# Hybrid block pair on one core: where the next head's query is split in a turn of the windowed attention

## The reference, cut to what matters

```python
def windowed_gqa_with_sink(q, k, v, sink):
    ...
    scores = jnp.einsum('bnqhrd,bnkhd->bnhrqk', qb, kb).astype(jnp.float32) * (ATTN_HEAD_DIM ** -0.5)
    ...
    scores = jnp.where(valid[None, :, None, None], scores, -jnp.inf)
    ...
    probs = jax.nn.softmax(jnp.concatenate([scores, sink_col], axis=-1), axis=-1)[..., :-1]
    out = jnp.einsum('bnhrqk,bnkhd->bnqhrd', probs.astype(v.dtype), vb)
```

## Time and profile before

| | |
|---|---|
| time, median of 3 runs | 2353.67 us (2353.35 to 2355.12) |
| time of the profiled execution | 2353.92 us |
| its span, first to last instruction | 2352.1 us |
| TensorE matmul busy | 2324.1 us, 99% |
| TensorE weight load busy | 2014.4 us, 86% |
| VectorE busy | 1636.3 us, 70% |
| ScalarE busy | 1243.7 us, 53% |
| GpSimd busy | 262.4 us, 11% |
| granted TensorE clock, mean | 0.999 |

### The profile page before, as it was taken

How to read it: one execution, slowest core, us unless ns; L and a number is a source line. 1 busy time by engine, 2 the same in 40 slices (tenths; PEclk the granted TensorE clock), 3 DMA queues, 4 the chain that set the end, 5 groups by cost and what they waited for, 6 DMA issues and landing times.

```text
span 2352.1 us, 35281 instructions
## 1 busy us (share of the span) xinstructions
PE 2324.1 (99%) x14088; PEld 2014.4 (86%) x14088; DVE 1636.3 (70%) x2353; ACT 1243.7 (53%) x2026; POOL 262.4 (11%) x208
## 2 busy tenths in 40 slices
PE   8999999999999999999999999999999999999998
PEld 7778778777788888899988899998887888899997
DVE  5698845478865455687785788785677565777784
ACT  7777765346663344455554555554544354555552
POOL 0000000465100100100002200001122201100002
PEclk9999999999999999999999999999999999999999
DMA  6221236324666232233233233223322232333222
GB/s 200 81 73 52 88 103 206 103 95 121 204 214 213 88 118 75 81 116 100 90 99 110 86 119 108 90 81 113 110 64 63 90 117 72 108 108 106 87 76 91
DMA packets 177844, 254.05 MB, mean 108 GB/s; under 512 B 10000, under 2 KB 101392, under 8 KB 177680
## 3 DMA queue, kind: packets, MB, share of 16 engines
q1 hardware_dynamic: 176528, 250.22, 33.1%
q10 hardware_dynamic: 1152, 1.57, 0.2%
HBM read 233.93 MB, written 16.78 MB: 107 GB/s over the span
## 4 chain that ended last, share of the span: by engine, by line
PE 93%; DVE 3%; ACT 2%; issue 1%; DMA 0%; POOL 0%; DVEq 0%; SPq 0%; POOLq 0%
PE bank L1492 92%; DVE wlo L2523 1%; PE bank L1660 1%; ACT whi L1899 0%; PE bank L1683 0%; PE bank L1781 0%; PE bank L1805 0%; DVE T L2531 0%; DVE W L2523 0%; DMA zb<-scr_z 0%; ACT E L2163 0%; DVE bank L2842 0%; DMA raw<-in_w_in 0%; PE bank L1618 0%; DVE xg L2527 0%
## 5 line engine op out<-in xcount | busy, mean ns | idle before, releaser
L1492 PE MATMUL bank<-xopr,shi 128*128 128x256 f32 x3360 | 605.0, 283 | 0.0
L1492 PEld LDWEIGHTS bank<-xopr,shi 128*128 128x128 f32 x3360 | 524.5, 192 | 0.5
L1492 PE MATMUL bank<-xopr,slo 128*128 128x256 f32 x1680 | 475.4, 283 | 0.0
L2523 DVE TENSOR_TENSOR wlo<-raw,whi 128x1024 fp32r<-128x1024 f32 (+2 forms) x286 | 354.6, 1244 | 140.8 <-ACT whi L1899 140.2
L1492 PE MATMUL bank<-xh,whi 128*128 128x512 f32 x1016 | 408.0, 402 | 7.4 <-DVE wlo L2523 7.4
L1492 PE MATMUL bank<-xh,wlo 128*128 128x512 f32 x1016 | 397.5, 391 | 0.0
L1492 PE MATMUL bank<-xl,whi 128*128 128x512 f32 x1016 | 397.2, 391 | 0.0
L1899 ACT ACTIVATE whi<-raw 128x1024 fp32r<-128x1024 f32 (+2 forms) x286 | 292.8, 1031 | 136.1 <-PE bank L1492 121.0
L1492 PEld LDWEIGHTS bank<-xopr,slo 128*128 128x128 f32 x1680 | 322.5, 192 | 0.0
L1492 PEld LDWEIGHTS bank<-xh,whi 128*128 128x128 f32 x1016 | 191.5, 188 | 50.0 <-DVE wlo L2523 8.2
L1492 PEld LDWEIGHTS bank<-xh,wlo 128*128 128x128 f32 x1016 | 191.1, 188 | 41.6
(11 more groups left out here) (398 smaller groups left out, 4320.7 us busy)
## 6 DMA issues: line engine op xcount, KB each, us to landing
raw<-in_w_in SPq DMA_DIRECT2D x92, 512.0 KB, 3.5
quarter<-in_w_ffn_in SPq DMA_DIRECT2D x32, 512.0 KB, 4.5
quarter<-in_ffn_gate SPq DMA_DIRECT2D x32, 512.0 KB, 3.6
quarter<-in_ffn_up SPq DMA_DIRECT2D x32, 512.0 KB, 4.6
raw<-in_ffn_down SPq DMA_DIRECT2D x28, 512.0 KB, 4.2
raw<-in_w_xattn_kv SPq DMA_DIRECT2D x16, 512.0 KB, 4.5
raw<-in_w_kv_mem SPq DMA_DIRECT2D x16, 512.0 KB, 4.9
raw<-in_w_branch_ssd SPq DMA_DIRECT2D x16, 512.0 KB, 4.6
```

The source lines that it names most:

```text
L1492: return e.matmul(out, l, r, start=start, stop=stop, skip_group_check=skip)
L2523: return e.tensor_tensor(out, a, b, op)
```

## The change

In each of the turns 0 to 14, the step `q_split(i + 1)` is taken out from behind `score_max(i, 1)` and `shift(i)` and put right behind `scores(i, 0)`. It stays the same step with the same instructions.

```diff
@@ -633,6 +633,8 @@
                         for r in (2 * pair, 2 * pair + 1):
                             side.new("sc", i, r)
                         step("scores", i, pair)
+                        if pair == 0 and i < 15:
+                            step("q_split", i + 1)
                     if i and pair == 0:
                         step("p_norm", last)
                     if i and pair:
@@ -644,8 +646,6 @@
                             step("shift", i)
                         elif i < 3:
                             step("k_split", i + 1)
-                    if pair and i < 15:
-                        step("q_split", i + 1)
                     if i:
                         side.new("pt", last, pair)
                         step("p_turn", last, pair)
```

## The result

The changed kernel takes 2356.86 us (median of 22 runs, 2355.25 to 2358.76). The kernel before takes 2353.84 us in 22 runs taken beside them. They reach from 2351.96 to 2355.12 us, with a single one far off at 3848.86 us, which can't move a median and which the ratio leaves out. The ratio is 1.0013, 95% interval 1.0007 to 1.0019: 1.6 to 4.5 us lost. That is real, and less than the 0.2% that I had set as the bound. The profiled execution took 2358.76 us, its span is 2356.1 us, and the clock's mean is 0.999.

What follows compares the result with a forecast made beforehand. TensorE's matmuls, busy 99% of the span, bound the kernel. Prices 0.83 + 0.75 + 0.41 + 0.83 + 0.38 = 3.2 us gave 2357.1 from the profiled execution, 2356.9 against the median; range 2353.9 to 2360.0.

Steps and rivals of the forecast that it cites:

- Turn 0: Attention's turn 0: ScalarE waits 6.18 us for TensorE behind the split's new place, which hides the split; no cost.
- Turn 1: Split ahead of ScalarE's normalisation delays it; transposition wait grows from 1.15 to 1.98 us, next stays 1.63; price 0.83 us.
- Turn 2: First maximum 1.58 us late, TensorE only 0.83, no room before second pair's scores; price 0.75 us, bounds 0 and 0.85.
- Turn 7: Transposition waiting for the normalisation: split costs 0.83, turn 6's removed split gives 0.42 back; price 0.41 us, bounds 0 and 0.83.
- Turn 10: Later normalisation delays VectorE's maximum; transposition's wait for its bank grows from 0.81 to 1.64 us; price 0.83, bounds 0 and 0.85.
- Turn 11: Same path as turn 10, 0.83 us late against 0.45 us of room at second pair's load; price 0.38, bounds 0 and 0.83.
- The other turns: Nine turns priced at nothing; hardest is turn 4, where 3.05 us of room hides VectorE's lag of 2.16 us.
- Slower: VectorE's waits for the high half exceed the room in turns 3 to 6, 8, 9: 5.1 us more, 2362.0; chance 0.18.
- Nothing to be seen on TensorE: Only turn 1's 0.83 us is lost; VectorE's gain behind shift covers the split at the other four places: 2354.5; chance 0.12.
- Faster: Earlier exponential and work behind it shrink the existing waits; at best 2349.7 us, short of 0.2%; chance 0.03.
- 3.97 us of existing waits: Weight-load idle times in the kernel before, in turns 1, 7 and 10: 1.15 + 1.63 + 0.38 + 0.81 us.
- The clock: Turn 1's wait of about 2 us drops TensorE's clock to 1.2 GHz, costing 5 us more: 2361.9; chance 0.02.

Runs made afterwards that it cites:

- ten_turns: Kernel before, with the split moved in turns 0, 3, 4, 5, 6, 8, 9, 12, 13 and 14 alone: 2353.40 us, ratio 0.9996.
- two_splits: Kernel before, with turn 1's split behind turn 0's first scores and turn 2's split behind shift(0): 2353.92 us, ratio 1.0001.
- five_turns: Kernel before, with the split moved in turns 1, 2, 7, 10 and 11 alone: 2358.22 us, ratio 1.0018.
- high_only: Kernel before, with only ScalarE's copies of the split moved in all 15 turns, VectorE's subtractions left behind shift: 2356.71 us, ratio 1.0010.
- two_ahead: Kernel before, with turns 1 and 2's splits in turn 0, turn 1's first maximum early, turn 0's normalisation directly behind its exponentials: 2356.04 us, ratio 1.0007.
- early_max: Kernel before, with only turn 1's first-pair maximum moved, right behind its scores: 2354.69 us, ratio 1.0003.
- behind_norm: Changed kernel, but with the split behind the normalisation instead of ahead of it: 2361.82 us (5 runs), ratio 1.0032.
- the last kernels: Kernel before with turns 1 and 2's splits in turn 0, without and with turns 6 and 9's splits also moved: 2353.92 and 2353.93 us.

## Why the prediction was right

**The time.** 2356.9 us predicted, 2356.86 measured. That they agree to 0.04 us is partly luck, since the medians of before themselves lie between 2353.67 and 2354.27. The sum is the better test: 3.20 us predicted, 3.27 in the ledger.

**Turn 0**, priced at nothing: its moved split is hidden, and even gives 0.13 us back at 87.36. ten_turns shows this alone (turn 0 moved, turn 1 not). two_splits puts a second split into turn 0, again at no cost.

**Turn 1**, 0.83 us: 0.86 by itself (five_turns), less turn 0's 0.13 gives the 0.73 in the table. The wait ahead of the transposition is 1.88 where I said near 2.0, the next one is unchanged as said. Behind it 0.13 us came back ahead of `scores(2, 0)`, where the wait for `pt` before `pv(0)` could shrink a little. I had left that out.

**Turn 2**, 0.75 us: 0.97, above my upper bound of 0.85. The maximum's delay was right: 109.65 against 107.38 less the start-up's 0.64 is 1.63 us, where I had 1.58. What I had too large was TensorE's own delay, which I set against it: 0.83, where the ledger stood at 0.73 - 0.13 = 0.60. The exponential waits 0.80 us for `shift` as I said. The cause is shown by high_only, where the subtractions stay and the jump is gone.

**Turn 7**, 0.41 us: 0.38, and both parts of the difference are shown: the split costs 0.81 alone (five_turns), and turn 6's moved subtractions give 0.43 back. In ten_turns, where only the giving back is left, it is worth 0.15, though the load idled 0.38. TensorE's matmuls in the kernel before say why:

```profile
202.03 0.39 PE L1492 MATMUL bank<-xl,whi 128*128 128x512 f32 x1
202.26 0.39 PE L1492 MATMUL bank<-xh,wlo 128*128 128x512 f32 x1
202.63 0.63 PE L1660 MATMUL bank<-cst,pr 128*128 128x128 f32 x4
```

The load idled beside a running matmul. The matmuls start 0.23 us apart, and this one came after 0.37: the wait was worth 0.14 us. The idle time of a load tells how a wait grows, but overstates what it costs. Turn 1's two waits, 1.15 and 1.63 us at the load:

```profile
86.22 0.39 PE L1492 MATMUL bank<-xh,wlo 128*128 128x512 f32 x1
87.36 0.63 PE L1660 MATMUL bank<-cst,pr 128*128 128x128 f32 x4 [0.75 <-ACT pr L1900]
...
90.35 0.39 PE L1492 MATMUL bank<-xh,wlo 128*128 128x512 f32 x1
91.98 0.58 PE L1492 MATMUL bank<-kh,qp 128*128 128x384 f32 x2 [1.24 <-DVE st L2663]
```

They are worth 87.36 - 86.22 - 0.23 = 0.91 us and 91.98 - 90.35 - 0.23 = 1.40 us, and two_ahead and early_max, which took them away, show just -0.90 and -1.40 in the ledger.

**Turn 10**, 0.83 us: 0.14 + 0.69 = 0.83. In five_turns the cost shows as a wait for a slot's low half instead (1.76 us at the load of 261.06, 0.75 at the same load before), of which 0.13 comes off the later wait: 1.02 - 0.13 = 0.89. I had said that a wait for low halves would come off the one at 266.68. **Turn 11**, 0.38 us: 0.29, the same in all three kernels that move ScalarE's copies in turns 10 and 11.

**The other turns**, nothing: turn 3 cost 0.23, which I had not foreseen, and ten_turns shows 0.14 there too. VectorE's gain of 0.85 us behind `shift(2)` was to cover the split. It ends in the wait of 1.08 us for `whi` in the rows above, where the kernel before has none: ScalarE writes this `whi` behind the exponentials, and these start from the same `shift`, so it comes no earlier. I had argued so for turn 2 and did not look for it in turn 3. In turn 4 VectorE waits 1.64 us, where I had worked out 1.31, and with the work of 0.85 the lag of 2.49 is still under the room of 3.05; no jump.

**The rivals.** *Slower:* its mechanism exists, as behind_norm shows with five such places, but not at this position of the split. *Nothing to be seen on TensorE:* excluded by five jumps. *Faster:* ten_turns and the last kernels show how little there is, 0.1 to 0.3 us, because a shortened wait comes back as another. My 3.97 us of existing waits could not be right beside the earlier trace rows, where TensorE idles 2.73 us in the whole stretch. Counted from matmul to matmul as in turn 7, the four waits are worth 0.91, 1.40, 0.14 and 0.55 us, 3.0 in all. The list of waits also lacked two, 0.49 us at 99.46 for `pt` and 0.75 us at 256.99 for a low half. *The clock:* it didn't fall in the changed kernel, behind the wait of 1.88 us or elsewhere up to the last matmuls. By the Trainium skill's page "TensorE: Matmul & The Clock Gate", in its part on the HAM clock gate, idleness brings the half clock back, and behind_norm and two_ahead agree with that, with 0.33 us for a load of 0.19. My price of 5 us for it was too high: the traces show 1.6 and 1.5 us (behind_norm's two falls) and 1.5 (two_ahead's).

## What to carry to other kernels

To price a move, look at what stands behind it on every engine up to the next idle time, and ask which of it TensorE waits for; work added there costs its full length, once, and in a gap nothing. Price a wait by how far apart the matmuls start around it, and not by the idle time of the weight load. Where a saturated engine sets the pace, a wait that you take away comes back a little later, and if waits flow together into one the clock may fall and make it a loss. For differences of a few microseconds in 2350, compare the start times of one engine's steps between two traces, and take the start-up off every time that you compare: with it, the copy that two_ahead brought 0.31 us forward reads as 0.86. Medians of eleven runs gave intervals of 2 us to either side; the ledger placed 0.1 us.

## What the runs showed of the hardware

TensorE's granted clock fell behind waits that I had thought harmless. After load waits of 2.50 us (behind_norm) and 2.55 us (two_ahead) it read 0.53 and 0.50 in the worst window of 2 us, the level of 1.2 GHz, and was back at 1.00 or 0.91 within 4 us. Each fall cost 1.5 to 1.6 us.

The length of the wait alone doesn't decide it. After 1.63 and 1.88 us (the changed kernel) and 1.92 (early_max) the clock read 1.00, and so it did behind the waits of 1.94 us at 533.58 and 1.95 at 641.29 in the changed kernel. But in behind_norm it fell once more behind waits of 1.84, 1.51 and 0.48 us, which every other trace here shows with the clock at 1.00. What else decides it stays open: no run here varied the wait alone.

The falls are not of the profiled executions only. The mean granted clock of a run reads 0.998 or 0.997 in all 5 runs of behind_norm and in 9 of the 11 of two_ahead, but in 5 and 4 of the 27 runs of the kernel before beside them; the others read 0.999. A profiled execution with one fall reads 0.998, one with two 0.997. How often the clock falls in the kernel before can't be told from this rounded number.
